# Chosen expert rows loaded in two parts, a norm per token tile and a later overflow test in a two-layer decoder trunk

## What is computed

```python
def rms_norm(x, g):
    xf = x.astype(jnp.float32)
    y = xf * lax.rsqrt(jnp.mean(xf * xf, axis=-1, keepdims=True) + EPS)
    return (y * g).astype(x.dtype)
...
    for l in range(DEPTH):
        ...
        h = rms_norm(x, norm_mix[l]) * (1.0 + sc1) + sh1
        gq, gk, gv, ga, gr, sq, sk, sv, mix_a, mix_b = split_columns(h @ w_in[l])
        ...
        y = moe_ffn(h2.reshape(B * S, D), w_router, b_router, w_gate[l], w_up[l], w_down[l])
        x = x + g2 * y.reshape(B, S, D)
```

## Time and profile before

| | us |
|---|---|
| median of 3 runs | 1649.22 |
| lowest and highest run | 1643.32, 1650.58 |
| the profiled execution, whole | 1645.64 |
| its span, first to last instruction | 1644.0 |
| PE busy in the span | 1456.7 (89%) |
| DVE, ACT, POOL busy | 980.7, 817.2, 197.0 |
| mean granted TensorE clock | 0.941 of full |

### The profile page before, as it was taken

One profiled execution on the slowest core, in us unless ns is written; L12 is line 12 of the kernel. 1 busy time (PEld: TensorE's weight loads), 2 busy tenths in 40 slices (PEclk: granted clock), 3 DMA queues, 4 the chain that ended last, 5 costly groups with the idle time before them and its releaser, 6 DMA issues.

```text
span 1644.0 us, 19335 instructions
## 1 busy us (share of the span) xinstructions
PE 1456.7 (89%) x7255; PEld 1146.7 (70%) x7256; DVE 980.7 (60%) x923; ACT 817.2 (50%) x1033; POOL 197.0 (12%) x186
## 2 busy tenths in 40 slices
PE   4999967999998999999859986799998999999592
PEld 2766855666677788888558784678787778888371
DVE  2435375232555899999561737433546789999083
ACT  2425233312144888888433523332324878887260
POOL 1000000000001133223110000000002033223021
PEclk9999679999999999999979977999999999999796
DMA  9665201567593899999532210022246699999164
GB/s 308 236 235 200 77 1 52 179 209 252 181 339 141 290 367 383 398 382 386 198 112 102 103 52 0 26 78 103 88 181 231 237 341 377 390 383 388 66 231 171
DMA packets 151012, 348.16 MB, mean 212 GB/s; under 512 B 10270, under 2 KB 12498, under 8 KB 149906
## 3 DMA queue, kind: packets, MB, share of 16 engines
q1 hardware_dynamic: 138866, 308.58, 51.9%
q0 software_dynamic: 12064, 38.46, 6.3%
HBM read 332.33 MB, written 23.59 MB: 217 GB/s over the span
## 4 chain that ended last, share of the span: by engine, by line
PE 66%; DVE 16%; ACT 5%; issue 4%; DMA 4%; DVEq 3%; SPq 1%; ACTq 0%; POOL 0%; POOLq 0%
PE PS L1058 18%; PE PS L1060 17%; PE PS L1059 17%; DVE ring_parts L1917 5%; PE PS L997 3%; ACT reg L910 2%; PE PS L1356 2%; PE PS L1168 2%; PE PS L1415 1%; PE PS L1198 1%; DMA ring<-in_w_ada 1%; DVEq L1685 1%; DMA reg<-y_rows 1%; PE PS L992 1%; DVE reg L1725 1%
## 5 line engine op out<-in xcount | busy, mean ns | idle before, releaser
L1059 PE MATMUL PS<-ring_parts,reg_parts 128*128 128x512 f32 x768 | 301.4, 392 | 0.0
L1058 PE MATMUL PS<-ring_parts 128*128 128x512 f32 (+1 forms) x704 | 275.6, 391 | 12.3 <-DVE hT_parts L1573 5.7
L1917 DVE TENSOR_TENSOR ring_parts<-ring,reg_parts 128x2048 fp32r<-128x2048 f32 x124 | 277.8, 2282 | 0.0
L925 ACT ACTIVATE reg_parts<-ring 128x2048 fp32r<-128x2048 f32 x124 | 226.8, 1901 | 1.5 <-DMA xs_rows<-reg 1.5
L1058 PE MATMUL PS<-reg_parts 128*128 128x512 f32 x504 | 204.1, 405 | 6.5 <-issue 3.1
L1565 DVE TENSOR_TENSOR ring_parts<-ring,ring_parts 128x2048 fp32r<-128x2048 f32 (+1 forms) x52 | 112.7, 2210 | 161.5 <-ACT ring_parts L773 161.5
L1060 PE MATMUL PS<-reg_parts 128*128 128x512 f32 x504 | 198.5, 394 | 0.0
L1058 PEld LDWEIGHTS PS<-ring_parts 128*128 128x128 f32 x704 | 132.7, 188 | 68.0 <-issue 33.9
L773 ACT ACTIVATE ring_parts<-ring 128x2048 fp32r<-128x2048 f32 (+1 forms) x52 | 93.3, 1845 | 159.9 <-DMA ring<-in_w_in 126.4
L1059 PEld LDWEIGHTS PS<-ring_parts,reg_parts 128*128 128x128 f32 x768 | 146.1, 190 | 28.4
L1917 DVE TENSOR_TENSOR ring_parts<-ring,hT_parts 128x2048 fp32r<-128x2048 f32 x64 | 146.2, 2287 | 11.1 <-issue 10.4
(11 more groups left out here) (304 smaller groups left out, 2192.1 us busy)
## 6 DMA issues: line engine op xcount, KB each, us to landing
ring<-in_w_up SPq DMA_DIRECT2D x32, 2048.0 KB, 16.4
ring<-in_w_gate SPq DMA_DIRECT2D x32, 2048.0 KB, 11.5
ring<-in_w_down SPq DMA_DIRECT2D x32, 2048.0 KB, 16.4
ring<-in_w_ada SPq DMA_DIRECT2D x40, 1024.0 KB, 5.3
ring<-in_w_in SPq DMA_DIRECT2D x16, 2048.0 KB, 7.8
ring<-in_w_ada SPq DMA_DIRECT2D x4, 2048.0 KB, 19.2
ring<-in_w_out SPq DMA_DIRECT2D x4, 2048.0 KB, 8.1
reg<-y_rows POOLq DMA_DIRECT2D x8, 1024.0 KB, 8.0
```

Of the source, the lines that this page charges most:

```text
L925: act.activation(w_high[part][:, cols], ring[:, 3 * k + part, cols], ACT.Copy).then_inc(w_hi[part], 1)
L1058: pe.matmul(out_, left[0], right[0], start=first, stop=False)
L1059: pe.matmul(out_, left[0], right[1], start=False, stop=False)
L1917: tt(ring_r[:, 3 * k + part, cols], ring[:, 3 * k + part, cols], w_high[part][:, cols].bitcast(F32), ALU.subtract).then_inc(w_lo[part], 1)
```

## The change

It does five things.

1. The router's index k of a chosen row is now the order of the expert number, not that of the score: k = 0 is the lower-numbered expert. So no row with k = 0 comes from expert 15.
2. GpSimd loads the rows with k = 0 (512 KB per tile) into half of `yc` as soon as expert 14's scatter has landed, ahead of its scatter of expert 15. SP loads the rows with k = 1 when that last scatter has landed. DVE adds all four tiles' first rows, then tile by tile the second ones.
3. TensorE's overflow test of expert 15 comes after down(14), DVE's after `finish(14)`. `gu_free` of the last expert is raised at the first transpose of its activation.
4. DVE's splits of units 0 and 1 stand ahead of `finish(15)`.
5. In the norm at a layer's start ACT takes a root per tile, its table is loaded ahead by a one-column root, DVE takes a reciprocal per tile, and TensorE transposes tile by tile, after 11 spare products that start with the first finished tile; before they were 20 and started with the third.

The cut diff leaves out the counts of semaphores, arguments that are passed on, and functions that only move.

```diff
--- before.py
+++ after.py
...
@@ -549,6 +554,9 @@
                     load(l + 1, W_SQ)
+                sp.wait_ge(y_stored[1], at(y_stored[1], l, 8 * E))
+                for t in range(NT):
+                    sp.dma_start(yc[t][:, 1, :], chosen_rows(t, 1)).then_inc(yc_loaded[t], 16)
                 sp.nop()
@@ -693,13 +701,12 @@
                     step(e, e % 2, (e - 1) // 2, more=False)
+                pool.wait_ge(gu_free, at(gu_free, l, E))
+                pool.wait_ge(y_stored[0], at(y_stored[0], l, 8 * E))
+                pool.wait_ge(y_stored[1], at(y_stored[1], l, 8 * E - 16))
+                for t in range(NT):
+                    pool.dma_start(yc[t][:, 0, :], chosen_rows(t, 0)).then_inc(yc_first, 16)
                 scatter(E - 1, 1, E // 2 - 1)
-                values = [in_register(at(y_stored[i], l, 8 * E)) for i in range(2)]
-                pool.wait_ge(pool_consts, 9)
-                for i in range(2):
-                    pool.wait_ge(y_stored[i], values[i])
-                for t in range(NT):
-                    pool.dma_start(yc[t], y_rows[2 * P * t:2 * P * (t + 1), :].rearrange("(p k) d -> p k d", k=TOPK)).then_inc(yc_loaded[t], 16)
                 value = in_register(at(x2_done, l, NT))
...
@@ -730,16 +743,11 @@
                                        accum_out=ss[:, t:t + 1])
-                    act.drain()
-                    act.activation(ss[:, :], ss[:, :], ACT.Sqrt, scale=1.0 / D, bias=eps).then_inc(root, 1)
+                        token_root(t)
 
                 def token_square(t):
                     act.wait_ge(x_done, at(x_done, l, NT + t + 1))
                     act.activation(xsq, xt[:, t, :], ACT.Square, accum_out=ss[:, t:t + 1])
-
-                def token_root(t):
-                    act.drain()
-                    act.activation(ss[:, t:t + 1], ss[:, t:t + 1], ACT.Sqrt, scale=1.0 / D, bias=eps).then_inc(root, 1)
 
...
@@ -784,8 +792,6 @@
                 else:
-                    split_high(0)
-                    split_high(1)
                     norm_tokens()
@@ -958,9 +964,9 @@
                         weights_high(pair_after, 1 - k, 1)
-                    if not isinstance(s, int) or s > 0:
-                        act.wait_ge(d_ready, at(d_ready, l, s))
                     if pair_after is not None:
+                        if not isinstance(s, int) or s > 0:
+                            act.wait_ge(d_ready, at(d_ready, l, s))
                         weights_high(pair, k, 2)
@@ -970,6 +976,9 @@
                 act.activation(o_aT, PS[:, 4, :].rearrange("p (f s) -> p f s", s=P), ACT.Copy).then_inc(t2_hi, 1)
+                if l < DEPTH - 1:
+                    split_high(0, l + 1)
+                    split_high(1, l + 1)
             act.wait_ge(x2_done, at(x2_done, DEPTH - 1, NT))
@@ -1038,10 +1047,10 @@
                 else:
-                    pe.wait_ge(x2_done, at(x2_done, l - 1, 3))
-                    spare_products(20, 4)
-                pe.wait_ge(xs_ready, at(xs_ready, l, NT))
+                    pe.wait_ge(x2_done, at(x2_done, l - 1, 1))
+                    spare_products(11, 4)
                 if l == 0:
+                    pe.wait_ge(xs_ready, at(xs_ready, l, NT))
                     transpose_tokens(range(6))
@@ -1051,7 +1060,12 @@
                 else:
-                    transpose_tokens(range(C))
+                    for t in range(NT):
+                        pe.wait_ge(xs_ready, at(xs_ready, l, t + 1))
+                        for k in range(C):
+                            mm = pe.transpose(PS[:, k, t * P:t * P + P], xs[:, t, k * P:k * P + P], ident[:, :])
+                            if t == NT - 1:
+                                mm.then_inc(ht_ready, 1)
 
...
@@ -1395,15 +1409,15 @@
 
-                def transposed_act(e, k):
+                def transposed_act(e, k, raise_at_first=None):
                     pe.wait_ge(act_done, at(act_done, l, e + 1))
-                    hidden(mact[k]).then_inc(t2_ready, 1)
-
-                def down(e, k, raise_at_first=None):
+                    hidden(mact[k], raise_at_first).then_inc(t2_ready, 1)
+
+                def down(e, k):
                     pe.wait_ge(t2_lo, at(t2_lo, l, e + 1))
                     pe.wait_ge(w_lo[2], at(w_lo[2], l, 2 * e + 2))
                     pe.wait_ge(y_done, at(y_done, l, e + 1))
-                    down_product(k, raise_at_first).then_inc(d_ready, 1)
+                    down_product(k).then_inc(d_ready, 1)
 
...
@@ -1447,18 +1461,18 @@
                     second_product(s, k)
-                    overflow(s, pair, k)
                     if more:
+                        overflow(s, pair, k, s)
                         transposed_tokens(s + 1, pair + k, 1 - k, gu_free)
-                        down(s - 1, 1 - k)
-                    else:
-                        down(s - 1, 1 - k, gu_free)
+                    down(s - 1, 1 - k)
+                    if not more:
+                        overflow(s, pair, k, s + 1)
 
                 with pe.Fori(0, E // 2 - 1) as j:
                     step(2 * j + 1, j, 1)
                     step(2 * j + 2, j + 1, 0)
                 step(E - 1, E // 2 - 1, 1, more=False)
-                transposed_act(E - 1, 1)
+                transposed_act(E - 1, 1, gu_free)
                 pe.wait_ge(t2_hi, at(t2_hi, l, E))
@@ -1530,12 +1544,11 @@
 
-                def norm_tokens():
-                    dve.wait_ge(root, at(root, l, 1))
-                    dve.reciprocal(rstd[:, :], ss[:, :])
+                def scale_tokens(t, rooted):
+                    dve.wait_ge(root, at(root, l, rooted))
+                    dve.reciprocal(rstd[:, t:t + 1], ss[:, t:t + 1])
                     dve.drain()
-                    for t in range(NT):
-                        ts(xs[:, t, :], xt[:, t, :], rstd[:, t:t + 1], None, ALU.mult).then_inc(xs_ready, 1)
+                    ts(xs[:, t, :], xt[:, t, :], rstd[:, t:t + 1], None, ALU.mult).then_inc(xs_ready, 1)
 
@@ -1547,7 +1560,8 @@
 
-                norm_tokens()
+                for t in range(NT):
+                    scale_tokens(t, t + 1)
                 dve.memset(attm[:, :, :, :], 0.0)
...
@@ -1859,9 +1867,16 @@
                 tt(sums[:, 3 * E:], sums[:, E:2 * E], sums[:, 3 * E:], ALU.add).then_inc(m_done, 1)
-                hots = rt[:, 3:5, :]
-                for k in range(TOPK):
-                    ts(hots[:, k, :], order_, float(k), None, ALU.is_equal)
+                hots, number_, last = rt[:, 3:5, :], rt[:, 5, :], rt[:, 6, 0:NT]
+                tt(number_.rearrange("p (t e) -> p t e", e=E), mask.rearrange("p (t e) -> p t e", e=E),
+                   e512.unsqueeze(1).broadcast_to([P, NT, E]), ALU.mult)
+                dve.drain()
+                dve.tensor_reduce(last, number_.rearrange("p (t e) -> p t e", e=E), AX.X, ALU.max)
+                dve.drain()
+                tt(hots[:, 1, :].rearrange("p (t e) -> p t e", e=E), number_.rearrange("p (t e) -> p t e", e=E),
+                   last.unsqueeze(2).broadcast_to([P, NT, E]), ALU.is_equal)
+                dve.drain()
+                tt(hots[:, 0, :], mask, hots[:, 1, :], ALU.subtract)
                 dve.drain()
...
@@ -1992,21 +2005,26 @@
                     step(2 * j + 4, 0, j + 1)
-                step(E - 1, 1, E // 2 - 1, more=False)
-                dve.wait_ge(y_stored[1], at(y_stored[1], l, 16 * (E // 2 - 1)))
-                finish(E - 1, 1)
-
+                hidden(E - 1, 1)
+                dve.wait_ge(y_stored[0], at(y_stored[0], l, 16 * (E // 2 - 1)))
+                finish(E - 2, 0)
+                overflow(E - 1)
                 if l < DEPTH - 1:
                     split_low(0, l + 1)
                     split_low(1, l + 1)
-
+                dve.wait_ge(y_stored[1], at(y_stored[1], l, 16 * (E // 2 - 1)))
+                finish(E - 1, 1)
+
+                def add_chosen(t, k):
+                    return stt(xt[:, t, :], yc[t][:, k, :], wts[:, k, t:t + 1], xt[:, t, :], ALU.mult, ALU.add)
+
+                dve.wait_ge(yc_first, at(yc_first, l, 16 * NT))
+                for t in range(NT):
+                    add_chosen(t, 0)
+                dve.drain()
                 for t in range(NT):
                     dve.wait_ge(yc_loaded[t], at(yc_loaded[t], l, 16))
-                    for k in range(TOPK):
-                        add = stt(xt[:, t, :], yc[t][:, k, :], wts[:, k, t:t + 1], xt[:, t, :], ALU.mult, ALU.add)
-                        if k == 0:
-                            dve.drain()
-                    add.then_inc(x2_done, 1)
+                    add_chosen(t, 1).then_inc(x2_done, 1)
 
```

## The result

| | kernel before | changed kernel |
|---|---|---|
| median of 5 runs | 1648.86 us | 1633.22 us |
| lowest and highest | 1643.32, 1650.58 | 1627.97, 1633.41 |
| the profiled execution | 1645.64 | 1633.41 |
| its span | 1644.0 | 1631.6 |

The ratio is 0.9907 with a 95% interval of 0.9887 to 0.9926: 15.6 us between the medians, where the prediction had 17.6 and a time of 1631.6.

A forecast was written before the change was run, and what follows sets the result against it. Bound by the exposed chain of scaling, scatter, loads and adds at the layer boundary and the end. 10.1 + 8.1 - 0.6 = 17.6 us, from 1649.2 to 1631.6; forecast case 1627 to 1636, 1623 to 1640 about 8 of 10.

The forecast's parts named there:

- Step 1: Overflow test behind down(14): layer 0's next transposes 1.9 us earlier (bounds 0.6 and 3.1); last layer 0.1.
- Rival (a): The moved overflow branch keeps its full price in both layers: +5.3 us, 1637; 15%.
- Step 2: Boundary, raw down product and splits: scaling of expert 15 0.7 us late, its scatter landing 3.41 after issue.
- Rival (c): First rows, 2 MB ahead on one queue, delay last scatter or first adds 3 us per layer: 1637.6; 8%.
- Step 3: GpSimd's first-choice loads at the boundary: landed 7.8 us after issue, adds inside DVE's wait, no cost.
- Step 4: SP's second-choice loads at the boundary: first tile 4.05 us after issue, last add at 831.7, 8.3 us gained.
- Step 5: Norm per tile at the boundary: first hT copy at 836.95 against 847.01, 10.1 us gained there in all.
- rival (b): Clock low when the next layer starts, slowing transposes and the first unit's products: 1634.6; 14%.
- The end of the span: Kernel's end: the last store closes the span, stores follow the adds as before; last add 8.1 us earlier.
- The router: Two compares become four dependent operations: costs 0.25 to 0.5 us per layer, 0.6 in all.
- Rival (e): Layer 1's expert loop: shifted code makes branches miss every pass, 39 us over 12 steps, 1671; 3%.
- The prediction's own signs of being wrong: Second add waiting for first rows, expert 15's scatter landing over 4 us after issue, splits over 1 us past raw product.

The follow-up runs named there:

- test_moved_alone: The kernel before with only expert 15's overflow test moved behind down(14), on TensorE and VectorE: 1647.25 us, ratio 0.9999.
- per_tile: The changed kernel with one wait and semaphore per tile of first rows instead of one wait for all four: 1633.53 us, ratio 0.9906.
- planes: The changed kernel with y_rows in two planes (row = 512 * choice + token), so a half load reads adjacent rows: 1633.59 us, ratio 0.9910.

## Why the prediction was right, and where it was off

- **Step 1, the test.** Down(14) came 7.08 us after the transposes of 14, exactly as forecast. The branch was mis-sized: I took a middle value for its price and an end 1.9 us earlier, but it took 2.93, near the price of the last layer, and ended with the product; in all nine profiles with the test behind down(14) in layer 0 it took 2.77 to 3.25. 3.0 us to the transposes (the upper bound, 3.1), 3.2 to the raw product. The cost sank because a product now runs above the branch, and the branch itself is shorter. By the Trainium skill's rule (Runtime: NRT & Kernel Launch, Instruction fetch mechanics) a branch out of the fetched pages waits for a fetch, so the wait would be moved and not removed; the row of 2925 ns behind down(14) agrees. In the last layer the moved branch cost 0.5 between the transposes (0.8 in test_moved_alone) instead of 0.1: 3.05 to 3.48 us there, not the 2.96 that I took over from the other place; 0.2 of it reached the raw product. Rival (a), the full price, never occurred behind down(14). Why the branch is shorter there is not isolated: its place and the DMA load changed together.
- **Step 2.** The scaling was 0.88 late, forecast 0.7. The scatter's landing, taken over as 3.41, was 4.05: 0.6 lost. In the last layer I had allowed 0.5 for data ahead of it; it took 5.00, 1.1 more than forecast to the landing. What failed here is the price of the overlap: the scatter lands with the first loads, 9.6 to 10.0 us behind their issue, and not 3.41 behind its own. Rival (c) was true in kind, at 0.6 and 1.1 us instead of 3; that the one queue is the reason, as it says, is not shown.
- **Step 3.** First rows landed 9.3 us behind the first issue instead of 7.8 (the 0.57 from a landing to the next issue, read from the earlier trace rows, is 0.60 there); per_tile shows that this cost nothing. The splits did not slow GpSimd's issues.
- **Step 4, the largest term.** From the landing of the scatter to the last add 10.15 instead of 9.2, and 9.93 instead of 9.6. The step that failed is the use of the earlier trace rows, weight loads of long rows, for loads that take every second row of 4 KB. In planes, with adjacent rows, it is still 9.62 and 9.84, so the pitch accounts for about 0.5 us at the boundary and 0.1 at the end, and the rest stays open.
- **Step 5** was right to 0.05 us: 5.20 from the last add to the first hT copy. The clock did fall, as rival (b) has it, though later: TensorE stood 2.89 us behind the transposes, and the granted clock was 0.5 from 844.7 to 851. The first products were paced by the hT copies, so the first evacuation of layer 1 came 4.89 us earlier than before where the first copy had come 5.05 earlier: 0.16 us.
- **The end of the span** was misread as the last store's. It was GpSimd's drain. 0.5 us of the gain there came from the drain, 3.50 instead of 4.07.
- **The router** was forecast at 0.6 in both layers; 0.16 is shown in layer 0. **Rival (e)** is out: the middle of layer 1 took 747.0 and 746.7 us from the first hT copy to the transposes of 14, against 747.3 and 749.3.

Boundary: 10.0 forecast, +1.3 from the branch, -0.15, -0.7 and -0.95 from splits, scatter and loads is 9.55. End: 8.1 forecast, -0.2, -1.1, -0.3 and +0.5 is 7.0. The second profiles of both kernels give 8.9 and 6.1. Less 0.3 for the routers, 14.6 to 16.2 us, and 15.6 by the medians. The prediction's own signs of being wrong all appeared, by small margins: the scatter of 15 landed 4.05 and 5.00 us after its issue (the limit was 4), DVE's splits ended 1.07 us past the raw product (the limit was 1), and the first add of second rows stood directly behind the four that had waited for first rows, though per_tile shows that this last cost nothing. So the time came out right while the scatter and the loads behind it did not go as described.

## What to carry to other kernels

Cut the chain at the boundary into intervals from one fixed event, and compare these, not absolute times: a profile whose upstream work is a few us early or late says nothing of the change. A transfer issued behind 2 MB that are still under way lands with them, so price its landing from the issue of those loads and not from its own. And ask of every engine, also one with nothing left to compute, when it reaches the closing barrier: a wait at the end of a program that protects nothing can hold up the end by itself.

## What the runs showed of the hardware

GpSimd's closing drain, started at the last add with all of GpSimd's own transfers landed, took the same time to the nanosecond in every kernel with the same last transfers: 4072 ns in the kernels that loaded full rows with four DMAs from GpSimd, 3501 with four loads of half rows, 6767 with none behind the last scatters. What it does is not shown; started earlier it took 8174 and 15161 ns and cost nothing. The same branch of TensorE took 5.2 to 5.5 us in front of down(14) in layer 0, where weight loads keep the DMA share at 1.0 all through it, and 2.7 to 3.5 in the last layer and behind down(14), where the share is mostly low or falls to 0 within some 3 us of the branch's start; after the idle time that it made in layer 0 the clock fell in four profiles and stayed up in one. Loads of every second 4 KB row ran at about half the rate of adjacent rows from their second to their fourth microsecond. And a scatter issued 4.4 to 6.4 us behind the first of four loads of 512 KB landed 9.6 to 10.0 us behind it at the boundary, on whichever queue these loads were.
